# A decoder layer on one core: the last pair of W_down column blocks done in two pieces by tokens, x1's transposes taken in pairs, one weight split moved

## The chip, the core and the metric

One core of a Trainium2 chip runs the whole layer in one launch. The metric is the device time in microseconds of one execution, the median of several runs. The engines are TensorE (PE, with its weight loads shown apart as PEld), VectorE (DVE), ScalarE (ACT), GpSimd (POOL) and SyncE (SP), each with its own instruction stream; they meet only at semaphores.

## The reference, cut to what matters

There are 256 prompt tokens and 8 x 8 sample tokens, 320 in all (TOK), a width of 2048 and a hidden width of 8192, everything in float32. The part that the change touches is the end of the layer:

```python
x = x + rmsnorm(mix, norm_post_mix[i])                                   # x1
hid = jnp.square(jax.nn.relu(rmsnorm(x, norm_pre_mlp[i]) @ w_up[i]))
x = x + rmsnorm(hid @ w_down[i], norm_post_mlp[i])                       # the outputs y_prompt, y_sample
```

`rmsnorm` divides each token by the root of the mean of its squares over all 2048 columns, so nothing of a token's output can be formed before every column of `hid @ w_down` is there for that token. Ahead of these lines stand the two head groups (an SSD scan and a convolution group) and `mix @ W_out`, which the change leaves alone.

## The kernel before

**Layout.** Activations lie transposed: 128 columns of the model on the partitions, a tile `t` (0 to 15) for each 128 columns, and the 320 tokens along the row. A float32 product is made of three float32r products of a high and a low part: `whi*hi`, `whi*lo`, `wlo*hi`. A weight block of 512 rows by 256 columns is loaded by SP into `raw`, rounded by ACT into `whi` (`split`, `ahead` on ACT), and its rest is formed by DVE in `wlo` (`ahead` on DVE). On PE a `granule` is such a block: two column tiles of 128, four row tiles, three matmuls each, 24 matmuls of 128x128 weights by 320 tokens. A pair of column tiles over K = 2048 (one quarter of the hidden width) is four granules (kq = 0 to 3), 96 matmuls. The MLP runs in four quarters of the hidden width; each has 8 pairs of W_up and 8 pairs of W_down, and DVE adds W_down's results into `ya`.

**The end.** The last pair (tiles 14 and 15) is done as 3 granules and then tile by tile over its last four row tiles (L2343 to L2345), with `tile_used` raised for each tile. DVE adds each tile to `ya` (L1796), ACT squares it into `sqm` (L1237), DVE adds the first to the sum of squares `acc2` (L1800), and PE forms the mean over the columns with one-column matmuls (`mean_rows`, L2351 and L2354), one for each block of 128 tokens and two for the 64 sample tokens. ACT takes the roots (L1240), DVE the reciprocals (L1834). `OUT_BLOCKS` is the order of the ten output blocks: (g, c) is 512 columns of the model by 128 tokens (c = 0, 1), or two column groups of the 64 sample tokens (c = 2). For each, PE turns four (or eight) tiles of the scaled result `yw` into token rows in a PSUM bank (`turn_out`, L2369, L2371), DVE multiplies by the reciprocal and adds x1 (L1838), and SP or ACT stores 256 KB, with c = 2 as two stores of 128 KB.

**The x1 stage.** After W_out and its norm (root `q1` by ACT), DVE forms x1 tile by tile in `mix` (L1720, L1724), ACT its high part `ahi` (L1157), DVE its low part `alo` (L1712). PE runs W_up's first two pairs row tile by row tile (`kk`), behind the transposes of the same x1 tile (`turn_x1`), which give x1's token rows that the end adds. Ahead of them PE issues nine 512-column products of data that it has already (L2248; nothing reads them). ACT copies each pair of turned tiles out of PSUM (`keep_rows`), and takes splits of coming weights in between. After the last tile DVE adds up squares, and with PE's mean (`rms_x1`) forms the second norm's `rb2`; the first hidden tiles follow from it.

Of the kernel before, what the change touches and what calls it, by code (L numbers as in the profile page):

```python
# [29 lines left out]
ALU = mybir.AluOpType  # L30
# [40 lines left out]
OUT_BANKS, COL_BANKS = (4, 5, 6, 0, 1, 2, 3), (7, 0, 1)  # L71
OUT_BLOCKS = ((0, 0), (0, 1), (1, 0), (1, 1), (0, 2), (2, 0), (2, 1), (3, 0), (3, 1), (2, 2))
# [36 lines left out]
def build(nc, x_prompt, x_sample, state_ssm, state_ssd_conv, state_conf, w_in, ssd_conv_w, ssd_conv_b,  # L109
# [3 lines left out]
    with ExitStack() as ctx:  # L113
# [237 lines left out]
        def _(sp):  # L351
# [89 lines left out]

            for k, (g, c) in enumerate(OUT_BLOCKS):
                if c == 0:
                    sp.wait_ge(out_done, k + 1)
                    sp.dma_start(y_prompt[0, 0:P, 512 * g:512 * g + 512], yo[:, 0, 512 * g:512 * g + 512]
                                 ).then_inc(y_out, 16)
                if c == 2:
                    sp.wait_ge(out_done, k + 1)
                    sp.dma_start(y_sample.rearrange("b s d -> (b s) d")[:, 512 * g:512 * (g + 1)],
                                 yo[0:64, 2, 512 * g:512 * g + 512]).then_inc(y_out, 16)  # L450
# [263 lines left out]
        def _(act):  # L714
# [492 lines left out]
            ahead(Q_MLP, 0, 6)  # L1207
# [27 lines left out]
            for n in range(2):  # L1235
                act.wait_ge(last_added, n + 1)
                act.activation(sqm[:, n, :], ya[:, NT - 2 + n, :], ACT.Square).then_inc(sqm_done, 1)  # L1237
            act.wait_ge(rms_mm, 3)
            for c in range(3):
                act.activation(scol[:, c:c + 1], ps[:, COL_BANKS[c], 0:1], ACT.Sqrt, bias=eps[:, 0:1]  # L1240
                               ).then_inc(col_root, 1)
            scaled(NT - 2)
            scaled(NT - 1)
            for k, (g, c) in enumerate(OUT_BLOCKS):
                if c == 1:
                    act.wait_ge(out_done, k + 1)
                    act.dma_start(y_prompt[0, P:SEQ, 512 * g:512 * g + 512], yo[:, 1, 512 * g:512 * g + 512]
                                  ).then_inc(y_out, 16)
                if c == 2:
                    act.wait_ge(out_done, k + 1)  # L1250
                    act.dma_start(y_sample.rearrange("b s d -> (b s) d")[:, 512 * (g + 1):512 * (g + 2)],
                                  yo[64:P, 2, 512 * g:512 * g + 512]).then_inc(y_out, 16)
# [8 lines left out]
        def _(dve):  # L1261
# [472 lines left out]
            for t in range(2, NT):  # L1734
                x1_part(t)
                x1_sum(t)
                if t == 2:
# [47 lines left out]

            def down(q, i, last=False):
                for c in range(8):
                    if not (last and c >= 6):
                        ahead(q_down(q), i, c)
                    if c % 4 == 3 and not (isinstance(q, int) and q == 0):  # L1790
                        p = c // 4
                        if last and p:
                            for n in range(2):
                                dve.wait_ge(tile_used, n + 1)
                                m = ya[:, NT - 2 + n, :]
                                dve.tensor_tensor(m, ps[:, 2 + n, 0:TOK], m, ALU.add).then_inc(last_added, 1)  # L1796
                                if n == 0:
                                    dve.wait_ge(acc_done, 3)
                                    dve.wait_ge(sqm_done, 3)
                                    dve.tensor_tensor(acc2[:, 0, :], acc2[:, 0, :], sqm[:, 0, :], ALU.add  # L1800
                                                      ).then_inc(acc_sum, 1)
                            return
# [28 lines left out]
            for k, (g, c) in enumerate(OUT_BLOCKS):  # L1831
                if k in (0, 1, 4):
                    dve.wait_ge(col_root, c + 1)
                    dve.reciprocal(rcol[:, c:c + 1], scol[:, c:c + 1]).then_inc(rcol_done, 1)  # L1834
                    dve.wait_ge(rcol_done, c + 1)
                dve.wait_ge(ot_trans, k + 1)
                rows_out = yo[:, c, 512 * g:512 * g + 512]
                dve.scalar_tensor_tensor(out=rows_out, in0=ps[:, OUT_BANKS[k % 7], :], scalar=rcol[:, c:c + 1],  # L1838
# [6 lines left out]
        def _(pe):  # L1845
# [414 lines left out]
            def turn_x1(t):  # L2260
                bank, n = (4 if t // 2 % 2 else 6), t % 2
                pe.wait_ge(xp_done, t + 1)
                if t == 2:
                    pe.wait_ge(rq_done, 2)
                if t >= 4 and n == 0:
                    pe.wait_ge(x1_rows, t // 2 - 1)
                for c in range(2):
                    pe.transpose(ps[:, bank, 256 * c + n * P:256 * c + (n + 1) * P], mix[:, t, c * P:(c + 1) * P],
                                 ident[:])
                last = pe.transpose(ps[0:64, bank + 1, n * P:(n + 1) * P], mix[:, t, SEQ:TOK], ident[:])  # L2270
                if n:
                    last.then_inc(x1_trans, 1)

            pe.wait_ge(read_dve, 16)
            pe.wait_ge(rooted, 7)
            for c in range(3):
                rows_c = min(P, TOK - c * P)
                last = pe.transpose(ps[0:rows_c, 5, c * P:(c + 1) * P], q1[:, c * P:c * P + rows_c], ident[:])
            last.then_inc(rq_trans, 1)
            for kq in range(4):  # L2280
# [3 lines left out]
                for k in range(4):  # L2284
                    kk = 4 * kq + k
                    turn_x1(kk)
# [43 lines left out]
            for i in range(1, 4):  # L2330
                for p in range(2):
                    pe.wait_ge(read_dve, 32 + 2 * i + p - 1)
                    for kq in range(4):
                        if i == 3 and p and kq == 3:
                            break
                        granule(q_down(3) + 2 * i + p, kq, 2 * p, hhi, hlo)

            pe.wait_ge(lo_done[3], q_down(3) + 8)
            for n in range(2):
                for k in range(4):  # L2340
                    kk = 12 + k
                    wh, wl = whi[:, 3, k, n * P:(n + 1) * P], wlo[:, 3, k, n * P:(n + 1) * P]
                    pe.matmul(ps[:, 2 + n, 0:TOK], wh, hhi[:, kk, :], start=False, stop=False)  # L2343
                    pe.matmul(ps[:, 2 + n, 0:TOK], wh, hlo[:, kk, :], start=False, stop=False)
                    last = pe.matmul(ps[:, 2 + n, 0:TOK], wl, hhi[:, kk, :], start=False, stop=(kk == NT - 1))  # L2345
                last.then_inc(tile_used, 1)


            def mean_rows(squares, first, stop):
                for c in range(2):  # L2350
                    pe.matmul(ps[:, COL_BANKS[c], 0:1], squares[:, c * P:(c + 1) * P], mean1[:, 0:1],  # L2351
                              start=first, stop=stop)
                for h in range(2):
                    last = pe.matmul(ps[64 * h:64 * h + 64, COL_BANKS[2], 0:1], squares[:, SEQ:TOK], mean1[:, 0:1],  # L2354
                                     start=first, stop=stop)
                return last

            def turn_out(k):
                g, c = OUT_BLOCKS[k]
                if k >= 7:  # L2360
# [54 lines left out]
```

## Time and profile before

| | |
|---|---|
| median of 3 runs | 1769.32 us (1769.3 to 1769.61) |
| the profiled execution, its own time | 1768.9 us |
| its span, first to last instruction | 1767.3 us |
| PE busy | 1755.0 us, 99% of the span, 13152 matmuls |
| DVE busy | 1080.9 us (61%) |
| ACT busy | 765.0 us (43%) |
| POOL busy | 451.9 us (26%) |
| granted TensorE clock, mean | 1.000 |

The time is about 1.6 us longer than the span. A matmul's busy time is its latency from start to end; matmuls overlap, so what one costs in a stream is the distance from start to start (or from end to end), and "PE 99% busy" doesn't say that PE is at its peak.

### The profile page before, as it was taken

How to read it: one execution, taken by the hardware profiler on the slowest of the kernel's cores; microseconds unless marked ns; L12 is line 12 of the kernel's file. 1: busy time of each engine (PE TensorE's matmuls, PEld its weight loads, DVE VectorE, ACT ScalarE, POOL GpSimd, SP SyncE). 2: the span in 40 equal slices, each digit the busy share in tenths (PEclk: the TensorE clock that was granted, in tenths of full speed). 3: DMA queues.
4: the chain of work that ended last, by engine and by line, in shares of the span. 5: the costliest groups of instructions: out<-in, count | busy, mean ns of one | idle time of the engine just before them, and what ended most of it. 6: DMA issues, size and time to landing. Idle time of an engine off the chain costs nothing.

```text
span 1767.3 us, 34687 instructions
## 1 busy us (share of the span) xinstructions
PE 1755.0 (99%) x13152; PEld 1732.5 (98%) x13152; DVE 1080.9 (61%) x1972; ACT 765.0 (43%) x1106; POOL 451.9 (26%) x347
## 2 busy tenths in 40 slices
PE   8999999999999999999999999999999999999998
PEld 7999999999999999999999999999999999999998
DVE  5587867999779788865854333444434434344444
ACT  7443435555348566533743333333233333333332
POOL 1577676777652112233100000000000000000232
PEclk9999999999999999999999999999999999999999
DMA  8665554555556777755444544444444444444742
GB/s 247 194 186 159 146 155 139 157 145 146 167 153 185 229 232 228 232 162 159 145 155 148 167 149 153 145 143 149 156 138 158 152 152 143 143 143 153 225 151 91
DMA packets 293608, 290.71 MB, mean 164 GB/s; under 512 B 12678, under 2 KB 287918, under 8 KB 292384
## 3 DMA queue, kind: packets, MB, share of 16 engines
q1 hardware_dynamic: 268008, 257.31, 47.9%
q10 hardware_dynamic: 22512, 19.23, 3.5%
q0 software_dynamic: 2992, 12.84, 2.3%
q8 instruction: 67, 1.10, 0.3%
q14 instruction: 29, 0.24, 0.0%
HBM read 270.85 MB, written 19.93 MB: 165 GB/s over the span
## 4 chain that ended last, share of the span: by engine, by line
PE 94%; DVE 3%; ACT 1%; issue 1%; DMA 0%; DVEq 0%; ACTq 0%
PE ps L1854 29%; PE ps L1856 28%; PE ps L1855 28%; DVE wlo L1266 1%; PE ps L2132 1%; PE ps L2148 1%; PE ps L2173 1%; PE ps L2167 1%; PE ps L2206 1%; PE ps L2208 1%; PE ps L2207 1%; PE ps L1942 0%; PE ps L1941 0%; PE ps L1940 0%; PE ps L2157 0%
## 5 line engine op out<-in xcount | busy, mean ns | idle before, releaser
L1854 PE MATMUL ps<-ahi,whi 128*128 128x320 f32 x2272 | 709.0, 312 | 0.5 <-DVE wlo L1266 0.5
L1856 PE MATMUL ps<-ahi,wlo 128*128 128x320 f32 x2272 | 703.1, 309 | 0.0
L1855 PE MATMUL ps<-alo,whi 128*128 128x320 f32 x2272 | 703.0, 309 | 0.0
L728 ACT ACTIVATE whi<-raw 128x1024 fp32r<-128x1024 f32 x463 | 478.5, 1055 | 399.3 <-PE ps L1856 378.7
L1266 DVE TENSOR_TENSOR wlo<-raw,whi 128x1024 fp32r<-128x1024 f32 x344 | 426.2, 1262 | 225.3 <-ACT whi L728 223.9
L1854 PEld LDWEIGHTS ps<-ahi,whi 128*128 128x128 f32 x2272 | 426.8, 188 | 2.8 <-DVE wlo L1266 0.8
L1855 PEld LDWEIGHTS ps<-alo,whi 128*128 128x128 f32 x2272 | 426.9, 188 | 0.5
L1856 PEld LDWEIGHTS ps<-ahi,wlo 128*128 128x128 f32 x2272 | 426.7, 188 | 0.0
L1856 PE MATMUL ps<-hhi,wlo 128*128 128x320 f32 x1016 | 314.5, 310 | 0.0
L1854 PE MATMUL ps<-hhi,whi 128*128 128x320 f32 x1016 | 314.5, 310 | 0.0
L1855 PE MATMUL ps<-hlo,whi 128*128 128x320 f32 x1016 | 314.4, 309 | 0.0
L539 POOL TENSOR_TENSOR wlo<-raw,whi 128x1024 fp32r<-128x1024 f32 x119 | 284.6, 2411 | 96.7 <-ACT whi L728 96.2
L1423 DVE SCALAR_TENSOR_TENSOR ps<-vx,par,ps 128x256 f32<-128x256 f32 (+1 forms) x928 | 290.7, 382 | 8.1 <-ACT vx L798 7.6
L692 POOL DMA_DIRECT2D yo<-x_rows x1 | 0.7, 737 | 757.5 <-PE ps L1856 757.5
L1855 PEld LDWEIGHTS ps<-hlo,whi 128*128 128x128 f32 x1016 | 190.8, 188 | 0.0
L1856 PEld LDWEIGHTS ps<-hhi,wlo 128*128 128x128 f32 x1016 | 190.8, 188 | 0.0
L1854 PEld LDWEIGHTS ps<-hhi,whi 128*128 128x128 f32 x1016 | 190.8, 188 | 0.0
L1173 ACT ACTIVATE hs<-rh 128x640 f32<-128x640 f32 x32 | 23.6, 739 | 205.3 <-DVE rh L1772 205.3
L1772 DVE SCALAR_TENSOR_TENSOR rh<-ps,rb 128x640 f32<-128x640 f32 x32 | 26.4, 824 | 136.2 <-PE ps L1856 136.2
L1805 DVE TENSOR_TENSOR ya<-ps,ya 128x640 f32 (+1 forms) x23 | 19.0, 824 | 111.0 <-PE ps L1856 111.0
L1775 DVE TENSOR_TENSOR hlo<-hs,hhi 128x640 f32 (+1 forms) x32 | 26.4, 825 | 57.4 <-ACT hhi L1175 57.4
L1854 PE MATMUL ps<-ghi,whi 128*128 128x320 f32 x192 | 59.3, 309 | 0.0
(334 smaller groups left out, 1604.2 us busy)
## 6 DMA issues: line engine op xcount, KB each, us to landing
raw<-in_w_in SPq DMA_DIRECT2D x144, 512.0 KB, 3.7
raw<-in_w_up SPq DMA_DIRECT2D x128, 512.0 KB, 4.3
raw<-in_w_down SPq DMA_DIRECT2D x128, 512.0 KB, 4.5
raw<-in_w_out SPq DMA_DIRECT2D x64, 512.0 KB, 4.2
h<-in_state_ssm ACTq DMA_DIRECT2D x16, 512.0 KB, 5.0
out<-hout SPq DMA_DIRECT2D x16, 512.0 KB, 3.8
wgt<-running_sums ACTq DMA_DIRECT2D x16, 320.0 KB, 5.4
x_transposed<-xt ACTq DMA_DIRECT2D x1, 2560.0 KB, 13.7
```

The lines of the kernel that those rows point to most:

```text
L539: pool.tensor_tensor(wlo[:, kq, :, :], raw[:, kq, :, :], whi[:, kq, :, :].bitcast(F32), ALU.subtract).then_inc(lo_done[kq], 1)
L728: act.activation(whi[:, kq, :, 0:width], raw[:, kq, :, 0:width], ACT.Copy).then_inc(hi_done, 1)
L1173: act.activation(hs[:], rh[:], ACT.Square).then_inc(hs_done, 1)
L1266: dve.tensor_tensor(wlo[:, kq, :, 0:width], raw[:, kq, :, 0:width], whi[:, kq, :, 0:width].bitcast(F32), ALU.subtract).then_inc(lo_done[kq ...
L1423: ins = dve.scalar_tensor_tensor(out=acc[s] if k else src[s], in0=src[s], scalar=par[:, j, R_CONV + k:R_CONV + k + 1], in1=acc[s], op0=ALU ...
L1772: dve.scalar_tensor_tensor(out=rh[:], in0=ps[:, bank:bank + 2, 0:TOK], scalar=0.0, in1=rbb, op0=ALU.max, op1=ALU.mult).then_inc(rh_done, 1)
L1775: dve.tensor_tensor(hlo[:, ds(4 * i + 2 * p, 2), :], hs[:], hhi[:, ds(4 * i + 2 * p, 2), :].bitcast(F32), ALU.subtract).then_inc(hid_ready, 1)
L1805: dve.tensor_tensor(m, gemm_bank(p), m, ALU.add).then_inc(read_dve, 1)
L1854: pe.matmul(out, wh, hi[:, kk, :], start=(kk == 0), stop=False)
L1855: pe.matmul(out, wh, lo[:, kk, :], start=False, stop=False)
L1856: last = pe.matmul(out, wl, hi[:, kk, :], start=False, stop=(kk == NT - 1))
L2132: last = pe.transpose(ps[:, 6 + b // 4, (b % 4) * P:(b % 4 + 1) * P], h0[:, j % 2, b, :], ident[:])
```

## The change

1. The last pair of W_down is done as two pieces. The first takes tokens 128 to 319 (192 of them, `EARLY`) over all four kq, the second tokens 0 to 127 (`LATE`) over all four kq, with the same weights loaded again. Sums, squares, mean and root are done for each piece. `OUT_BLOCKS` is put in another order: blocks of the early tokens first. The early tokens' mean and the blocks k = 0, 1, 2 are put between the late piece's kq, block 3 and the late mean behind it.
2. `turn_x1` takes two tiles at the odd `kk`, and `q1`'s transposes go from ahead of `kk` = 0 to ahead of `kk` = 1. DVE's two reciprocals for them move from tile 2 to tile 3.
3. ACT's split number 6 of W_up goes from behind the tile loop to its last tile, ahead of `keep_rows(6)`.

```diff
-OUT_BANKS, COL_BANKS = (4, 5, 6, 0, 1, 2, 3), (7, 0, 1)
-OUT_BLOCKS = ((0, 0), (0, 1), (1, 0), (1, 1), (0, 2), (2, 0), (2, 1), (3, 0), (3, 1), (2, 2))
+OUT_BANKS, COL_AT = (4, 5, 6, 2, 3, 4, 5, 6, 0, 1), (16, 0, 8)
+OUT_BLOCKS = ((0, 1), (1, 1), (2, 1), (0, 2), (3, 1), (0, 0), (1, 0), (2, 0), (2, 2), (3, 0))
+LATE, EARLY = slice(0, P), slice(P, TOK)
...
+                if t == NT - 1:
+                    ahead(Q_MLP, 0, 6)
                 if t % 2 and t >= 3:
                     keep_rows(t // 2 - 1)
...
-            ahead(Q_MLP, 0, 6)
             ahead(Q_MLP, 0, 7)
...
+            last_squares(0)
+            for k in range(3):
+                store_rows(k)
+            last_squares(1)
+            store_rows(6)
+            store_rows(9)
...
+            def last_part(h):
+                cols = (EARLY, LATE)[h]
+                for n in range(2):
+                    dve.wait_ge(tile_used, 2 * h + n + 1)
+                    m = ya[:, NT - 2 + n, cols]
+                    dve.tensor_tensor(m, ps[:, (2, 0)[h] + n, cols], m, ALU.add).then_inc(last_added, 1)
+                    if n == 0:
+                        dve.wait_ge(acc_done, 3)
+                        dve.wait_ge(sqm_done, 3 + 2 * h)
+                        dve.tensor_tensor(acc2[:, 0, cols], acc2[:, 0, cols], sqm[:, 0, cols], ALU.add
+                                          ).then_inc(acc_sum, 1)
...
-            pe.wait_ge(rooted, 7)
-            for c in range(3):
-                rows_c = min(P, TOK - c * P)
-                last = pe.transpose(ps[0:rows_c, 5, c * P:(c + 1) * P], q1[:, c * P:c * P + rows_c], ident[:])
-            last.then_inc(rq_trans, 1)
...
-                    turn_x1(kk)
+                    if kk == 1:
+                        turn_q1()
+                    if kk % 2:
+                        turn_x1(kk // 2)
                     pe.wait_ge(ahi_done, 2 * NT + kk + 1)
...
+            def last_piece(h, kq):
+                cols = (EARLY, LATE)[h]
+                for n in range(2):
+                    out = ps[:, (2, 0)[h] + n, cols]
+                    for k in range(4):
+                        kk = 4 * kq + k
+                        wh, wl = whi[:, kq, k, n * P:(n + 1) * P], wlo[:, kq, k, n * P:(n + 1) * P]
+                        pe.matmul(out, wh, hhi[:, kk, cols], start=(kk == 0), stop=False)
+                        pe.matmul(out, wh, hlo[:, kk, cols], start=False, stop=False)
+                        last = pe.matmul(out, wl, hhi[:, kk, cols], start=False, stop=(kk == NT - 1))
+                    if kq == 3:
+                        last.then_inc(tile_used, 1)
...
+            pe.wait_ge(read_dve, 32 + 6)
+            for kq in range(4):
+                pe.wait_ge(lo_done[kq], q_down(3) + 8)
+                last_piece(0, kq)
+            pe.wait_ge(read_dve, 32 + 7)
+            last_piece(1, 0)
+            mean_rows(0)
+            last_piece(1, 1)
             turn_out(0)
             turn_out(1)
+            last_piece(1, 2)
             turn_out(2)
+            last_piece(1, 3)
+            turn_out(3)
+            pe.wait_ge(col_root, 2)
+            mean_rows(1)
+            for k in range(4, 10):
                 turn_out(k)
```

PE's stream at the end of the program before, from the last W_down matmul on; a row is a line of the code, the operation, out<-in, the output's shape and what it waits for.

```order
L2345 MATMUL ps<-hhi,wlo 128x320
L2351 MATMUL ps<-mean_95,acc_133 128x1 [waits acc_sum]
L2351 MATMUL ps<-mean_95,acc_133 128x1
L2354 MATMUL ps<-mean_95,acc_133 64x1 x2
L2369 MATMUL ps<-ident,ywa 128x128 [waits yw_done]
L2369 MATMUL ps<-ident,ywa 128x128 x3
L2351 MATMUL ps<-mean_95,sqm 128x1 [waits sqm_done]
L2351 MATMUL ps<-mean_95,sqm 128x1
L2354 MATMUL ps<-mean_95,sqm 64x1 x2
L2369 MATMUL ps<-ident,ywa 128x128 x8
L2369 MATMUL ps<-ident,ywa 128x128 [waits col_root,last_added]
```

The same stream of the changed kernel, where the late piece (128 tokens) ends.

```order
L2371 MATMUL ps<-hhi,wlo 128x128
L2402 MATMUL ps<-ident,ywa 64x128 [waits last_added]
L2402 MATMUL ps<-ident,ywa 64x128 x7
L2381 MATMUL ps<-mean_95,acc_133 128x1 [waits sqm_done,acc_sum,col_root]
L2381 MATMUL ps<-mean_95,sqm 128x1
L2400 MATMUL ps<-ident,ywb 128x128 [waits yw_done]
L2400 MATMUL ps<-ident,ywb 128x128 x3
L2400 MATMUL ps<-ident,ywa 128x128 [waits out_done]
L2400 MATMUL ps<-ident,ywa 128x128 x3
```

Four output blocks (k = 0 to 3) and the early tokens' mean are issued before the late mean; behind it stand the six blocks 4 to 9, where before all ten stood behind or beside the one mean.

PE's stream at the start of the x1 stage, before the change.

```order
L2248 MATMUL ps<-ghi 128x512 x8
L2278 MATMUL ps<-ident,q_138 128x128 [waits rooted,read_dve]
L2278 MATMUL ps<-ident,q_138 128x128
L2278 MATMUL ps<-ident,q_138 64x128
L2268 MATMUL ps<-ident,mix 128x128 [waits xp_done,lo_done1,lo_done0]
L2268 MATMUL ps<-ident,mix 128x128
L2270 MATMUL ps<-ident,mix 64x128
L2293 MATMUL ps<-ahi,whi 128x320 [waits ahi_done]
```

The same place in the changed kernel; left out at the dots are the rest of the first W_up matmuls (`kk` = 0), which alternate L2318 and L2319.

```order
L2267 MATMUL ps<-ghi 128x512 x8
L2318 MATMUL ps<-ahi,whi 128x320 [waits lo_done1,ahi_done,lo_done0,read_dve]
...
L2324 MATMUL ps<-alo,whi 128x320 x3
L2298 MATMUL ps<-ident,q_138 128x128 [waits rooted]
L2298 MATMUL ps<-ident,q_138 128x128
L2298 MATMUL ps<-ident,q_138 64x128
L2289 MATMUL ps<-ident,mix 128x128 [waits xp_done]
```

The six transposes that stood between the nine products and the first W_up matmul are now behind `kk` = 0, so that this matmul's wait for `ahi` stands right behind the nine products.

ACT's stream after the last x1 tile, before the change.

```order
L1143 ACTIVATE sqx<-mix 128x1280
L1151 ACTIVATE rows_86<-ps,sx 128x256 [waits rq_done,x1_trans]
L1151 ACTIVATE rows_86<-ps,sx 128x256
L1152 ACTIVATE rows_86<-ps,sx 64x256
L728 ACTIVATE whi<-raw 128x1024 [waits raw_ready0,weights_used,pst_out,hout_out]
L728 ACTIVATE whi<-raw 128x1024 [waits weights_used,raw_ready1]
```

And in the changed kernel: the first of the two splits has gone ahead of the three row copies.

```order
L1147 ACTIVATE sqx<-mix 128x1280
L732 ACTIVATE whi<-raw 128x1024 [waits weights_used,raw_ready0]
L1155 ACTIVATE rows_86<-ps,sx 128x256 [waits rq_done,x1_trans]
L1155 ACTIVATE rows_86<-ps,sx 128x256
L1156 ACTIVATE rows_86<-ps,sx 64x256
L732 ACTIVATE whi<-raw 128x1024 [waits raw_ready1,weights_used,pst_out,hout_out]
```

## Rows read from the trace of the kernel before

**Rows 1.** The page: span, and PE's busy time, share, instructions.

```profile
span 1767.3 us, 34687 instructions
PE 1755.0 (99%) x13152; PEld 1732.5 (98%) x13152; DVE 1080.9 (61%) x1972; ACT 765.0 (43%) x1106; POOL 451.9 (26%) x347
```

**Rows 2.** The page: the chain that ended last, by engine.

```profile
PE 94%; DVE 3%; ACT 1%; issue 1%; DMA 0%; DVEq 0%; ACTq 0%
```

**Rows 3.** PE's timeline, last pair's kq 3, matmul 1 and 24: start, duration.

```profile
1750.00 0.31 PE L2343 MATMUL ps<-hhi,whi 128*128 128x320 f32 x1
...
1753.37 0.31 PE L2345 MATMUL ps<-hhi,wlo 128*128 128x320 f32 x1
```

**Rows 4.** Weight loads: timeline, then groups (mean ns), then one line's (min/median/max).

```profile
1753.61 0.52 PEld L2351 LDWEIGHTS ps<-mean,acc 128*128 128x128 f32 x4 [0.19 <-DVE acc L1800]
...
L1854 PEld LDWEIGHTS ps<-hhi,whi 128*128 128x128 f32 x1016 | 190.8, 188 | 0.0
...
L2268 PEld LDWEIGHTS ps<-ident,mix x32: 138/140/144, 845.2 to 876.6; 128*128 128x128 f32 x32
...
L1885 PEld LDWEIGHTS ps<-zeros,identb x36: 97/132/152, 3.3 to 14.6; 128*128 128x128 bf16 x36
```

**Rows 5.** Line L2116: loads and matmuls with 64 moving columns, ns min/median/max.

```profile
L2116 PEld LDWEIGHTS ps<-xb,pad x8: 192/192/193, 547.2 to 686.3; 128*128 128x128 f32 x8
L2116 PE MATMUL ps<-xb,pad x8: 222/248/276, 547.3 to 686.4; 128*128 128x64 f32 x8
```

**Rows 6.** PE's timeline behind the last W_down matmul.

```profile
1753.61 0.61 PE L2351 MATMUL ps<-mean,acc 128*128 128x1 f32 x4
1754.14 0.28 PE L2354 MATMUL ps<-mean,acc 128*64 128x1 f32 x4
1754.36 0.66 PE L2369 MATMUL ps<-ident,ywa 128*128 128x128 f32 x4
...
1756.98 1.58 PE L2371 MATMUL ps<-ident,ywa 128*64 128x128 f32 x16
```

**Rows 7.** DVE's timeline there: last add, first reciprocal, last six blocks.

```profile
1753.72 0.49 DVE L1796 TENSOR_TENSOR ya<-ps,ya 128x320 f32<-128x320 f32 x1 [0.17 <-PE ps L2345]
1756.00 0.16 DVE L1834 RECIPROCAL rcol<-scol 128x1 f32<-128x1 f32 x1 [1.78 <-ACT scol L1240]
...
1759.22 4.04 DVE L1838 SCALAR_TENSOR_TENSOR yo<-ps,rcol,yo 128x512 f32<-128x512 f32 x6
```

**Rows 8.** Stores: the first two (1756 to 1758), the last two (from 1763.2).

```profile
out<-yo SPq DMA_DIRECT2D x1, 256.0 KB, 2.3
...
out<-yo SPq DMA_DIRECT2D x1, 128.0 KB, 3.0
out<-yo ACTq DMA_DIRECT2D x1, 128.0 KB, 3.6
```

**Rows 9.** Start of the x1 stage: PE's first transposes, ACT's first tile.

```profile
845.01 0.49 PE L2278 MATMUL ps<-ident,q 128*128 128x128 f32 x3
...
844.80 0.56 ACT L1157 ACTIVATE ahi<-mix,par 128x320 fp32r<-128x320 f32 x1 [0.20 <-DVE mix L1724]
```

**Rows 10.** PE's one wait after the x1 stage.

```profile
900.76 0.31 PE L1856 MATMUL ps<-ahi,wlo 128*128 128x320 f32 x1
901.58 0.41 PE L1854 MATMUL ps<-ahi,whi 128*128 128x320 f32 x1 [0.51 <-DVE wlo L1266]
```

**Rows 11.** ACT after its last x1 tile, and what DVE waits for there.

```profile
874.47 0.81 ACT L1151 ACTIVATE rows<-ps,sx 128x256 f32<-128x256 f32 x2
...
875.54 2.00 ACT L728 ACTIVATE whi<-raw 128x1024 fp32r<-128x1024 f32 x2
...
876.62 1.23 DVE L1266 TENSOR_TENSOR wlo<-raw,whi 128x1024 fp32r<-128x1024 f32 x1 [1.23 <-ACT whi L728]
```

**Rows 12.** The second norm's mean on PE and DVE's step that needs it.

```profile
882.24 1.24 PE L2257 MATMUL ps<-sqx,mean 128*128 128x320 f32 x4
...
884.41 0.49 DVE L1760 SCALAR_TENSOR_TENSOR qq<-qq,ps 128x320 f32<-128x320 f32 x1
```

More of the change, by code:

```diff
@@ L1792, in down @@
                         if last and p:
[L1793 to L1801, printed above, removed]
+                            last_part(0)
                             return
@@ L2258, in rms_x1, with turn_x1, turn_q1 @@
                 last.then_inc(rms_mm, 1)
[L2260 to L2263, printed above, removed]
+            def turn_x1(r):
+                bank = 4 if r % 2 else 6
+                pe.wait_ge(xp_done, 2 * r + 2)
+                if r == 1:
                     pe.wait_ge(rq_done, 2)
[L2265 to L2272, printed above, removed]
-            pe.wait_ge(read_dve, 16)
-            pe.wait_ge(rooted, 7)
-            for c in range(3):
-                rows_c = min(P, TOK - c * P)
-                last = pe.transpose(ps[0:rows_c, 5, c * P:(c + 1) * P], q1[:, c * P:c * P + rows_c], ident[:])
-            last.then_inc(rq_trans, 1)
+                if r >= 2:
+                    pe.wait_ge(x1_rows, r - 1)
+                for n in range(2):
+                    t = 2 * r + n
+                    for c in range(2):
+                        pe.transpose(ps[:, bank, 256 * c + n * P:256 * c + (n + 1) * P], mix[:, t, c * P:(c + 1) * P],
+                                     ident[:])
+                    last = pe.transpose(ps[0:64, bank + 1, n * P:(n + 1) * P], mix[:, t, SEQ:TOK], ident[:])
+                last.then_inc(x1_trans, 1)
+            def turn_q1():
+                pe.wait_ge(rooted, 7)
+                for c in range(3):
+                    rows_c = min(P, TOK - c * P)
+                    last = pe.transpose(ps[0:rows_c, 5, c * P:(c + 1) * P], q1[:, c * P:c * P + rows_c], ident[:])
+                last.then_inc(rq_trans, 1)
+            pe.wait_ge(read_dve, 16)
             for kq in range(4):
@@ L2330, in _ @@
             for i in range(1, 4):
-                for p in range(2):
+                for p in range(2 if i < 3 else 1):
                     pe.wait_ge(read_dve, 32 + 2 * i + p - 1)
                     for kq in range(4):
-                        if i == 3 and p and kq == 3:
-                            break
                         granule(q_down(3) + 2 * i + p, kq, 2 * p, hhi, hlo)
[L2338 to L2346, printed above, removed]
@@ L2349, in mean_rows @@
[L2349 to L2356, printed above, removed]
+            def last_piece(h, kq):
+                cols = (EARLY, LATE)[h]
+                for n in range(2):
+                    out = ps[:, (2, 0)[h] + n, cols]
[7 more added lines that the diff above has]
+                        last.then_inc(tile_used, 1)
@@ new lines, in mean_rows @@
+            def mean_rows(h):
+                pe.wait_ge(acc_sum, h + 1)
+                pe.wait_ge(sqm_done, 4 + 2 * h)
+                for c in ((1, 2), (0,))[h]:
+                    for rows in ((slice(0, P),) if c < 2 else (slice(0, 64), slice(64, P))):
+                        for squares, first in ((acc2[:, 0, :], True), (sqm[:, 1, :], False)):
+                            last = pe.matmul(ps[rows, 7, COL_AT[c]:COL_AT[c] + 1], squares[:, c * P:min(c * P + P, TOK)],
+                                             mean1[:, 0:1], start=first, stop=not first)
+                last.then_inc(rms_mm, 1)
@@ L2358, in turn_out @@
             def turn_out(k):
                 g, c = OUT_BLOCKS[k]
[L2360 to L2361 removed]
+                if k in (3, 8):
+                    pe.wait_ge(last_added, 2 if k == 3 else 4)
+                if k in (5, 6, 7):
+                    pe.wait_ge(out_done, k - 4)
+                if k in (0, 4, 9):
+                    pe.wait_ge(yw_done, {0: 12, 4: NT, 9: NT + 2}[k])
                 for h in range(2 if c == 2 else 1):
@@ L2365, in turn_out @@
                         rows, lo = (slice(0, P), c * P) if c < 2 else (slice(64 * h, 64 * h + 64), SEQ)
-                        out = ps[rows, OUT_BANKS[k % 7], n * P:(n + 1) * P]
+                        out = ps[rows, OUT_BANKS[k], n * P:(n + 1) * P]
                         tile = yw[t // 12][:, t % 12, lo:lo + rows.stop - rows.start]
```

75 lines of the change are left out of this document (33 added, 42 removed).

## The prediction

> **What bounds the kernel now.** I read the page's head first, then the chain that ended last, then timelines of the two stretches that the change touches. PE is busy 99% of the span with 13152 matmuls, each with a weight load of its own [rows 1], and 94% of the chain is PE's, 3% DVE's [rows 2]. So an edit is worth what it adds to or takes from PE's stream, plus what it does in two places where PE isn't the bound: behind the last W_down matmul, and at the one wait after the x1 stage. The last pair's stream has no gap: the 24 matmuls of kq 3 start from 1750.00 to 1753.37, (1753.37 - 1750.00)/23 = 0.1467 us apart, for 320 columns [rows 3]; the pair's 96 take 14.08 us.
>
> **Part 1a, the pair's stream.** The change makes 192 matmuls of these 96: 96 with 192 columns, 96 with 128. It moves the same number of columns, but loads each weight tile twice. If only columns cost, 0.1467 us falls in proportion, to 0.088 and 0.0587 us, and the sum is 14.08 us again. The other bound is the weight load. The mean's matmuls have one column, so nothing of theirs streams, and yet their four loads of 128 columns start 0.11 us apart: (0.52 - 0.19)/3 [rows 4]. A second place has 64 moving columns behind 128-column weights [rows 5]: of its two matmuls the first takes 222 ns, its weights loaded behind a longer matmul, the second 276, 54 ns more, which is the load that it waits for. Both places have plain float32 weights, and the pair's are float32r; but a load of `whi` takes 188 ns, as theirs do (190 and 192), while the loads of the transposes take 140 [rows 4, 5]. At 320 columns a load of 0.11 us is hidden under 0.147 us; at 192 (0.088) and at 128 (0.059) it isn't. I take 0.110 us for both widths, since those rows are the nearest: one has fewer columns than either piece, and the price didn't fall. 192 x 0.110 = 21.1 us against 14.08: **+7.0 us**. Bounds: 0 (columns alone) and, if a narrow matmul kept the whole 0.1467 us, 28.2 - 14.1 = +14.1 us.
>
> The Trainium skill, "TensorE: Matmul & The Clock Gate", section "Weight-path perf modes", says that weights of 128 columns that are not FP32 are read in four parallel chunks, for a load of some 32 cycles. If float32r counted as such, the first term would be 0 and not +7.0 us. The trace speaks against it: bf16 loads took as little as 97 ns, the float32r loads 188 [rows 4]. Its section "Back-to-back issue gap" gives a sustained 81 ns per matmul of 128 columns; by that the term would be an estimated 96 x (0.088 + 0.081) - 14.08 = +2.1 us. No row here shows a 128-column load that quick in a stream.
>
> **Part 1b, what is put between.** The early tokens' mean comes before the late kq 1: four instructions with 128-column weights (1753.61 to 1754.14, 0.53 us) and eight with 64-column ones, whose four took 0.22 us (1754.14 to 1754.36) [rows 6], so 0.44: **+1.0 us**. Blocks 0, 1, 2 are twelve transposes; three `q` ones took 0.49 us with 0.27 for the last [rows 9], so 0.11 each: **+1.3 us**. These ran behind the last W_down matmul before, in DVE's shadow; now they delay it. Waits inside the pieces: the early results are added about 0.35 us after their last matmul, and squares and sums (0.5 us each at 320 columns [rows 7]) finish some 1.5 us into the late kq 0, which takes 24 x 0.11 = 2.6 us. So PE shouldn't wait, and DVE, which is otherwise idle there, does blocks 0 to 2 under the pieces. If that cover went, the wait would be under 1 us. Loads for the pair are split long before. Sum of 1a and 1b: the last W_down matmul starts 9.3 us later relative to the pair's start.
>
> **Part 1c, the tail.** Let T be the start of that last matmul. Before, the last block ends at 1759.22 + 4.04 = 1763.26 with T = 1753.37: T + 9.9 [rows 3, 7]. After: block 3 (16 instructions, 1.58 us [rows 6]) runs from T + 0.15, so PE is free at T + 1.7. The adds and squares of 128 columns are done by then (T + 0.35, then two steps of about 0.3 us and PE's notice: about T + 1.1). The late mean is only 4 instructions, 0.53 us: T + 2.3. Root and reciprocal: T + 2.8. Block 4 needs no late root; its transposes come behind the late mean, T + 2.8, and DVE does it from T + 2.95. Then five blocks: six in a row took 4.04 us, 0.74 for the last, so 0.66 each [rows 7]. With the reciprocal (0.2) between blocks 4 and 5, DVE would end at T + 7.2. Block 8 (sample tokens, 1.6 us of PE) ends its turning about T + 5.8, which costs DVE some 0.15 more. End T + 7.35: **-2.5 us**. Bounds -3.2 (no wait on PE) and -2.0 (each turn late).
>
> Then the drain: from 1763.26 to the span's end 4.04 us. The last stores took 3.0 and 3.6 us to land, the first only 2.3 [rows 8]: the ten blocks' 2.6 MB queue up. After, four blocks are stored earlier, but the last six still come each 0.66 us, so most of the queue stays: **-0.3 us** (0 to -0.9).
>
> **Parts 2 and 3, the x1 stage.** Before, PE starts `q1`'s transposes at 845.01 and x1's behind them [rows 9], work that fills the time until `ahi`'s first tile is there, 844.80 + 0.56 = 845.36. After, the first thing behind the nine products is the matmul that needs this tile: PE starts at about 845.42, 0.4 us late, with all the same work to do. Pairing the transposes saves nothing that I can price. But the chain then goes through DVE and ACT, not PE: at 901.58 PE starts after a wait for `wlo`; it had been ready at 900.76 + 0.147 = 900.91, so 0.67 us was idle [rows 10]. A PE that is 0.4 us late has only 0.27 idle left, if the chain stays. And part 3 shortens the chain: DVE waited 1.23 us for the split that ACT began at 875.54, behind row copies from 874.47 [rows 11]; ahead of them it is 1.07 us sooner. DVE's step at 884.41 needs the mean of which the last of 4 instructions ends at 882.24 + 1.24 = 883.48 [rows 12], 883.9 with PE's delay, so 0.5 us of that is kept. The `wlo` is then ready at 901.08, PE at 901.32, and PE sets it: 901.58 becomes 901.3, **-0.3 us**. Bounds: -0.7 (no idle and no delay), +0.4 (the chain not shortened and PE pushed on in full). Row copies end later by the split's 1.07 us, about 876.6; PE needs them only after the tile loop. Alone, the x1 edits would be within 0.2%.
>
> **The sum.** +7.0 + 1.0 + 1.3 - 2.5 - 0.3 - 0.3 = +6.2 us. Against the profiled execution's own time, 1768.9 us, that is 1775.1. The median of the runs is 0.4 us above that execution, so I predict 1775.5 us, 0.35% slower. A measurement of this kernel tells about 0.2% (3.5 us) from no change.
>
> **The rivals.**
>
> A, the weight load hides or is cheap: pairs stay at the column price, term 1a is 0, and the time is 1775.5 - 7.0 = 1768.5 us, not slower. For it: streams here have no visible load cost at 320 columns, and float32r isn't shown narrow in any row. Against it: rows 4 and 5. It decides if the mean distance of the 192 matmuls is under 0.096 us (192 x 0.0958 = 18.4; less 14.1 and less 0.8 of the other terms is 3.5 us). To be faster by 0.2% it would need the best bounds of tail, drain and x1 stage as well, and cheaper fillers (-0.7, -0.6, -0.4 from 1768.5 is 1766.8, still inside 0.2%). By the 81 ns of the Trainium skill's page on TensorE the time would be an estimated 1775.5 - 7.0 + 2.1 = 1770.6 us. Chance 0.11, of which 0.03 faster.
>
> B, a narrow float32r matmul costs no less than a wide one (0.1467 us), from load and stream not overlapping well: 1775.5 + 7.1 = 1782.6 us. For it: nothing is seen at these widths. Against: one column or 64 cost 0.11 in all. Chance 0.06.
>
> C, the forecast: load-bound at 0.107 to 0.115 us, and the other terms within their bounds: 1773.5 to 1777.5 us. Chance 0.83.
>
> **How the numbers follow.** Range 1772.5 to 1780.5 us: it holds C with a margin for fillers or waits that I have wrong, and the way up towards B (a distance of up to 0.135 us); A is left out. Faster 0.03, same 0.09, slower 0.88.
>
> **What would show it.** In the trace after: the 192 matmuls' starts (or ends) 0.11 us apart in both pieces, and 21 us for the 192 where they are back to back; if the 128-column ones are quicker than the 192-column ones, A is right in part. The last W_down matmul some 9 us later, the last block 7.4 us behind it. PE starting W_up at 845.4 with an idle stretch behind the nine products, and no wait near 901. Wrong above all would be the load's price for float32r, which the trace has only under wide matmuls; next the count of what is hidden behind the late mean.

## The result, and the profile after

The changed kernel takes 1776.57 us, median of 6 runs (1775.52 to 1779.09), against 1769.51 us before in the same session (1769.3 to 1770.13): ratio 1.0043, with a 95% interval of 1.0032 to 1.0054 (the ratios are the recorded ones and need not be the quotient of the medians, here 1.0040). It is slower, as predicted (1775.5, range 1772.5 to 1780.5). Three of the six executions took 1775.52 to 1775.69 us, at a mean granted clock of 1.000, and three 1777.45 to 1779.09, at 0.998 to 0.996. Executions that were disturbed as a whole (two of e2's twelve, at 1891 and 4433 us, and one of the kernel before, at 3483 us) are left out of every comparison. The profiled execution took 1775.52 us. It stands 6.6 us above the profiled one of before; the sum had +6.2.

The page of the changed kernel, head and chain, answers to [rows 1, 2]:

```profile
span 1773.7 us, 34887 instructions
PE 1762.3 (99%) x13248; PEld 1739.7 (98%) x13248; DVE 1081.8 (61%) x1975; ACT 765.9 (43%) x1110; POOL 451.9 (25%) x347
...
PE 98%; DVE 1%; DMA 0%; ACT 0%; issue 0%; SPq 0%; DVEq 0%
```

PE has 96 matmuls more and is busy 7.3 us longer, in a span that is 6.4 us longer. The chain is now 98% PE's: DVE's share at the end and near 901 us has shrunk, and PE's own stream has grown by more.

The two pieces. First the windows (PE, PEld, DVE, ACT, POOL busy, granted clock, DMA share, GB/s): the early piece, then the late one with what is put between.

```profile
1739.29:1749.95 10.66, 10.66 (x98) 10.66 (x97) 3.83 (x5) 2.42 (x5) 5.38 (x3) 1.00 0.01 2
1750.00:1762.72 12.72, 12.72 (x122) 12.69 (x121) 3.35 (x8) 1.77 (x6) 0.00 (x0) 1.00 0.17 63
```

Then the groups by shape (busy us, mean ns of one):

```profile
L2370 PE MATMUL ps<-hlo,whi 128*128 128x128 f32 x32 | 8.8, 274 | 0.0
L2370 PE MATMUL ps<-hlo,whi 128*128 128x192 f32 x32 | 8.8, 274 | 0.0
```

PE never pauses, at the full clock, and a matmul of 128 columns lasts as long as one of 192 (274 ns). The starts tell what one costs. These are the first and the last matmul of the early piece, then the first and the 24th of the late one:

```profile
1739.31 0.25 PE L2369 MATMUL ps<-hhi,whi 128*128 128x192 f32 x1
...
1749.90 0.27 PE L2371 MATMUL ps<-hhi,wlo 128*128 128x192 f32 x1
1750.01 0.24 PE L2369 MATMUL ps<-hhi,whi 128*128 128x128 f32 x1
...
1752.55 0.27 PE L2371 MATMUL ps<-hhi,wlo 128*128 128x128 f32 x1
```

(1749.90 - 1739.31)/95 = 0.111 us for 192 columns and (1752.55 - 1750.01)/23 = 0.110 us for 128, two thirds of the columns; the median distance is 0.111 us in both pieces. For [rows 3] it was 0.1467 us.

PE's timeline at the end, from the last W_down matmul, answers to [rows 6]:

```profile
1762.72 0.27 PE L2371 MATMUL ps<-hhi,wlo 128*128 128x128 f32 x1
1762.92 1.58 PE L2402 MATMUL ps<-ident,ywa 128*64 128x128 f32 x16
1764.43 0.38 PE L2381 MATMUL ps<-mean,acc 128*128 128x1 f32 x2
1764.68 0.36 PE L2381 MATMUL ps<-mean,sqm 128*128 128x1 f32 x2
1764.90 0.63 PE L2400 MATMUL ps<-ident,ywb 128*128 128x128 f32 x4
1765.37 1.47 PE L2400 MATMUL ps<-ident,ywa 128*128 128x128 f32 x12
```

And DVE's there, which answers to [rows 7]:

```profile
1763.03 0.29 DVE L1803 TENSOR_TENSOR ya<-ps,ya 128x128 f32<-128x128 f32 x1 [0.31 <-PE ps L2371]
1763.24 0.15 DVE L1853 RECIPROCAL rcol<-scol 128x1 f32<-128x1 f32 x1
1764.61 0.75 DVE L1857 SCALAR_TENSOR_TENSOR yo<-ps,rcol,yo 128x512 f32<-128x512 f32 x1 [1.22 <-PE ps L2402]
1765.57 0.75 DVE L1857 SCALAR_TENSOR_TENSOR yo<-ps,rcol,yo 128x512 f32<-128x512 f32 x1 [0.21 <-PE ps L2400]
1766.24 0.15 DVE L1853 RECIPROCAL rcol<-scol 128x1 f32<-128x1 f32 x1
1766.43 3.38 DVE L1857 SCALAR_TENSOR_TENSOR yo<-ps,rcol,yo 128x512 f32<-128x512 f32 x5
```

With T = 1762.72 the last block ends at 1766.43 + 3.38 = 1769.81, T + 7.09 (before T + 9.9). The reader can see the plan work as meant: block 3 covers adds and squares (1762.92 to 1764.4), the late mean has only four matmuls, and six blocks are left behind it. The span ends 3.9 us after the last block. The last stores (KB each, median us to landing) are as slow as those of [rows 8]:

```profile
out<-yo SPq DMA_DIRECT2D x2, 128.0 KB, 3.3
...
out<-yo ACTq DMA_DIRECT2D x1, 256.0 KB, 3.5
```

Counted from the pair's start (1739.31 us, before 1739.44), the spans differ by the last W_down matmul 9.5 us later, a tail shorter by 2.8, a drain shorter by 0.1, and 0.1 from the x1 stage: 6.4 us.

The x1 stage: PE's timeline at its start and where the wait of [rows 10] was.

```profile
845.57 0.39 PE L2318 MATMUL ps<-ahi,whi 128*128 128x320 f32 x1 [0.35 <-ACT ahi L1161]
...
901.41 0.31 PE L1875 MATMUL ps<-ahi,wlo 128*128 128x320 f32 x1
901.55 0.31 PE L1873 MATMUL ps<-ahi,whi 128*128 128x320 f32 x1
```

And DVE's timeline where it waited 1.23 us before [rows 11], and at the step of [rows 12]:

```profile
876.19 1.23 DVE L1278 TENSOR_TENSOR wlo<-raw,whi 128x1024 fp32r<-128x1024 f32 x1 [0.16 <-ACT whi L732]
...
884.24 0.49 DVE L1772 SCALAR_TENSOR_TENSOR qq<-qq,ps 128x320 f32<-128x320 f32 x1 [0.30 <-PE ps L2276]
```

PE is idle 0.35 us behind the nine products, and the matmuls near 901 follow each other at 0.147 us with no wait. DVE's wait for the split has gone from 1.23 to 0.16 us, but its step at 884.24 comes only 0.17 us sooner than before, since it now waits for PE's mean.

### The profile page after: what moved, and what is told of

Same layout as the page of the kernel before. It is cut to its first block, busy times and chain, and to the rows that moved or that the text cites. A ratio compares the mean times of both kernels' runs of the same rounds, so it can differ in the third digit from the quotient of the medians.

```text
span 1773.7 us, 34887 instructions
## 1 busy us (share of the span) xinstructions
PE 1762.3 (99%) x13248; PEld 1739.7 (98%) x13248; DVE 1081.8 (61%) x1975; ACT 765.9 (43%) x1110; POOL 451.9 (25%) x347
## 4 chain that ended last, share of the span: by engine, by line
PE 98%; DVE 1%; DMA 0%; ACT 0%; issue 0%; SPq 0%; DVEq 0%
PE ps L1873 29%; PE ps L1874 29%; PE ps L1875 29%; PE ps L2151 1%; PE ps L2167 1%; PE ps L2192 1%; PE ps L2186 1%; PE ps L2318 1%; PE ps L2225 1%; PE ps L2324 1%; PE ps L2226 1%; PE ps L2227 1%; PE ps L2319 1%; PE ps L1961 0%; PE ps L1959 0%; PE ps L1960 0%
## 5 line engine op out<-in xcount | busy, mean ns | idle before, releaser
L1873 PE MATMUL ps<-hhi,whi 128*128 128x320 f32 x992 | 306.5, 309 | 0.0
L1874 PE MATMUL ps<-hlo,whi 128*128 128x320 f32 x992 | 306.5, 309 | 0.0
L1875 PE MATMUL ps<-hhi,wlo 128*128 128x320 f32 x992 | 306.5, 309 | 0.0
L1873 PEld LDWEIGHTS ps<-hhi,whi 128*128 128x128 f32 x992 | 186.2, 188 | 0.0
L1874 PEld LDWEIGHTS ps<-hlo,whi 128*128 128x128 f32 x992 | 186.2, 188 | 0.0
L1875 PEld LDWEIGHTS ps<-hhi,wlo 128*128 128x128 f32 x992 | 186.2, 188 | 0.0
L1875 PE MATMUL ps<-ghi,wlo 128*128 128x320 f32 x192 | 59.2, 308 | 0.0
```

Of the source, the lines that this page charges most:

```text
L1873: pe.matmul(out, wh, hi[:, kk, :], start=(kk == 0), stop=False)
L1874: pe.matmul(out, wh, lo[:, kk, :], start=False, stop=False)
L1875: last = pe.matmul(out, wl, hi[:, kk, :], start=False, stop=(kk == NT - 1))
```

## The experiments

The first three take the change apart.

**e1: part 1 alone** (the two pieces and the new order of the end; x1 stage and split as before).

> Part 1 alone (pieces, tail), the x1 stage as before. Load theory: the whole loss is here, +6.2 to +6.7 us on before, about 1776 us where the granted clock is full; 192 narrow matmuls 0.111 us apart. Rival, the x1 edits cost something of their own: then this is nearer to before, under +5 us. On the executions of the changed kernel that had a mean granted clock of 0.996 to 0.998: if the clock falls because of the narrow stretch, they turn up here and not in e2; if it falls because of PE's idle stretch at 845 us, they turn up in e2 and not here.

Measured: 1776.66 us (1775.65 to 1783.96, 6 runs), ratio 1.0049 (1.0036 to 1.0063), the changed kernel's time. Span 1774.2 us, tail T + 7.1, and the wait near 901 is there as before. All of the loss is in part 1. So are the executions with a lower mean clock: three of the six lie above 1777 us, at 0.994 to 0.998, as three of the changed kernel's do, while the ten of e2 all lie between 1768.72 and 1769.54 us.

**e2: parts 2 and 3 alone** (the x1 stage and the split; the end as before).

> Parts 2 and 3 alone (pairs of transposes, split moved), the end as before. Forecast of the prediction: PE starts W_up 0.4 us late and no longer waits near 901 us: -0.1 to -0.3 us, 1769.2 to 1769.4, not to be told from no change. Rival: the x1 stage carries part of the +6 us; then over +1 us here.

Measured: 1769.25 us (10 runs) against 1769.55, ratio 0.9999 (0.999 to 1.0008), not to be told from no change. PE idles 0.33 us ahead of 845.47, and the wait near 901 is gone. The expected -0.3 us was met, but the next two runs show that its parts weren't.

**e3: part 3 alone.**

```diff
+                if t == NT - 1:
+                    ahead(Q_MLP, 0, 6)
                 if t % 2 and t >= 3:
                     keep_rows(t // 2 - 1)
...
-            ahead(Q_MLP, 0, 6)
             ahead(Q_MLP, 0, 7)
```

> Part 3 alone (the split one place sooner). Chain theory: DVE's steps from 876 us on come 0.5 to 1.0 us sooner, PE is not late, so its idle 0.67 us at 901 us shrinks to under 0.2: -0.5 us, about 1769.0. Rival: the mean at 882 us, which PE gives when it gets there, holds DVE anyway and only 0.4 to 0.5 us comes out; or nothing, if another wait takes its place.

Measured: 1768.57 us (1768.05 to 1768.87, 11 runs) against 1769.55, ratio 0.9995 (0.9986 to 1.0004). DVE's timeline in it:

```profile
883.65 0.49 DVE L1761 SCALAR_TENSOR_TENSOR qq<-qq,ps 128x320 f32<-128x320 f32 x1 [0.28 <-PE ps L2258]
...
899.53 4.63 DVE L1267 TENSOR_TENSOR wlo<-raw,whi 128x1024 fp32r<-128x1024 f32 x4
```

The step of [rows 12] comes 0.76 us sooner and is then held by PE, the `wlo` at 899.53 as much sooner (before 900.30), and PE doesn't wait any more: its 0.67 idle microseconds are all saved, and the span is 1766.6 us, 0.7 shorter. The medians differ by 0.98 us; where the other 0.3 us lies isn't shown. It is the fastest kernel of this study, below both others, though its interval doesn't tell it from no change.

**e6: part 2 alone** (transposes in pairs, `q1`'s behind `kk` = 0; split 6 where it was).

```diff
+                    if kk == 1:
+                        turn_q1()
+                    if kk % 2:
+                        turn_x1(kk // 2)
-                    turn_x1(kk)
```

> Part 2 alone (transposes of x1 in pairs, q1's behind the first row tile). PE 0.4 us late at 845 us; the chain of DVE and ACT unchanged, so the wait near 901 us shrinks from 0.67 to about 0.3 us and the time stays: 0.0 us. Rival: the delay is passed on in full, +0.4 us; or pairing saves on PE, -0.2 us or more.

Measured: 1769.98 us (1769.39 to 1770.58, 11 runs) against 1769.4, ratio 1.0003 (0.9994 to 1.0012): +0.6 us, where nothing was expected; the interval doesn't tell it from no change. The profiled span grew by 0.5 us, and the traces show how. ACT's timeline, first of this kernel:

```profile
854.28 1.06 ACT L728 ACTIVATE whi<-raw 128x1024 fp32r<-128x1024 f32 x1 [0.60 <-PE ps L2305]
```

then of the kernel before:

```profile
853.64 1.06 ACT L728 ACTIVATE whi<-raw 128x1024 fp32r<-128x1024 f32 x1
```

And PE's timeline of this kernel, where the wait of [rows 10] was at 901.58:

```profile
902.22 0.41 PE L1854 MATMUL ps<-ahi,whi 128*128 128x320 f32 x1 [0.51 <-DVE wlo L1266]
```

PE begins the row tile `kk` = 3 at 852.47 us, 0.63 us later than before (851.84), and not 0.4; 0.07 of that was there ahead of the stage. The delayed PE frees its weights later, ACT's split waits for that (0.60 us, where it didn't wait before), and everything that ACT and DVE do from there is 0.64 us later, down to the `wlo` at 900.94 (before 900.30). So PE's delay doesn't eat its idle time near 901: the chain moves with it, and the wait stays 0.5 us long.

The next two measure the price of a narrow matmul.

**e4: each of 92 of the pair's 96 matmuls issued as two, 192 and 128 columns, with the same weights right behind each other**; everything else as before.

```diff
+                        for w, h in ((wh, hhi), (wh, hlo), (wl, hhi)):
+                            first, end = kk == 0 and w is wh and h is hhi, kk == NT - 1 and w is wl
+                            for cols in ((slice(0, TOK),) if first or end else
+                                         (slice(0, WIDTHS[kq]), slice(WIDTHS[kq], TOK))):
+                                last = pe.matmul(ps[:, 2 + n, cols], w, h[:, kk, cols],
+                                                 start=first, stop=end)
```

> The kernel before, with 92 of the last pair's 96 matmuls each issued as two that follow one another with the same weights, 192 and 128 columns; nothing else is changed, results are the same. Load theory: 184 x 0.111 + 4 x 0.147 - 14.1 = +6.9 us, about 1776.4. Rival 1, columns are the price: 0. Rival 2, a repeated weight tile is not loaded again: about 0 as well, or half of it (92 loads fewer). Rival 3, the loss of the change comes from what is put between the pieces and from the tail: 0 here.

Measured: 1776.38 us (1776.01 to 1776.69, 5 runs), ratio 1.004 (1.0026 to 1.0053); the last W_down matmul 7.2 us later (7.0 counted from the pair's start), the tail 9.9 us as before. The price goes with the number of matmuls and their loads, whatever the order, and weights that are already there are loaded and paid for again: the trace has 92 weight loads more than before.

**e5: the same with other widths, one for each kq**: 256 + 64, 192 + 128, 160 + 160, 288 + 32.

```diff
-            WIDTHS = (192, 192, 192, 192)
+            WIDTHS = (256, 192, 160, 288)
```

> As e4, but the split of the columns differs by kq: 256+64, 192+128, 160+160, 288+32. Load theory, a matmul starts no sooner than 0.111 us after the one before, and no sooner than 0.000458 us a column: 256 gives 0.117, 288 gives 0.132, all others 0.111 (64 and 32 too). Column theory: 0.029 for 64, 0.015 for 32. A theory of a fixed cost per matmul on top of the columns: 0.088 + x and 0.059 + x differ in the same granule, which the load theory says they don't. Its time (about 1776.8) is of no interest.

Measured: 1777.4 us (one run). From the starts, two matmuls of a pair together take 227, 223, 223 and 244 ns. In groups by shape (the mean of one is its latency):

```profile
L2349 PE MATMUL ps<-hhi,whi 128*128 128x160 f32 x16 | 3.1, 276 | 0.0
...
L2349 PE MATMUL ps<-hlo,whi 128*128 128x288 f32 x8 | 3.0, 379 | 0.0
...
L2349 PE MATMUL ps<-hlo,whi 128*128 128x64 f32 x8 | 1.5, 192 | 0.0
...
L2349 PE MATMUL ps<-hhi,whi 128*128 128x32 f32 x8 | 1.4, 178 | 0.0
```

A matmul costs the larger of its columns (0.1467/320 = 0.458 ns each) and 111 ns. For 192 + 128 and 160 + 160 that is 2 x 111 = 222 ns, for 256 + 64 it is 117 + 111 = 228, for 288 + 32 it is 132 + 111 = 243. A price by columns (147 ns for every pair) falls, and so does a fixed extra for each matmul, which would make all pairs equal. A least distance between the starts of any two matmuls falls too: behind a matmul of 32 columns the next one starts 26 to 30 ns later. It is the starts of the weight loads that are never less than 0.108 us apart here. That the number of weight columns sets this shows in [rows 6], for plain float32: four matmuls with 64-column weights took 0.22 us, 0.055 each, half of the 0.11 with 128.

**e7: the split by tokens in the last kq only** (48 narrow matmuls for 24 wide ones, the early mean inside, all ten blocks behind; parts 2 and 3 as in the changed kernel).

> The split by tokens only in the last kq of the last pair: 48 narrow matmuls in place of 24 wide ones, kq 0 to 2 at 320 columns; early mean between the late piece's two tiles, ten output blocks behind the last matmul. Load theory: 48 x 0.111 - 3.5 = +1.8 us in place of +7.2; mean +1.0; the tail ends about 8 us behind the last matmul's start in place of 9.9: sum +0.9 us, 1770.4. Rival, the loss is in the tail's order and the work between: then this is as slow as the change, +4 us or more.

Measured: 1770.81 us (1770.52 to 1773.55, 11 runs), ratio 1.0011 (1.0002 to 1.002). Counted from the pair's start, the last W_down matmul is 2.7 us later (48 x 0.111 - 24 x 0.1467 = 1.8, and the mean's 0.8), the tail 1.1 us shorter. Even a quarter of the split costs more than it gives back. Two of the 11 executions stand apart, at 1773.16 and 1773.55 us, with a mean clock of 0.998 and 0.997; neither was profiled.

**e8: the changed kernel with blocks 0 to 2 behind the last matmul** and not between the late kq.

```diff
             last_piece(1, 1)
+            last_piece(1, 2)
+            last_piece(1, 3)
             turn_out(0)
             turn_out(1)
-            last_piece(1, 2)
             turn_out(2)
-            last_piece(1, 3)
```

> The changed kernel with output blocks 0 to 2 turned behind the last matmul and not between the late pieces. If doing them early gains what the prediction says: the last matmul starts 1.4 us sooner than in the changed kernel, the tail grows by 1.6 us (three blocks of DVE, 0.66 each, less what PE's turning of block 3 and the late mean left idle): +0.2 us on the changed kernel. Rival, they are a net loss where they stand: 1 us faster than the changed kernel. Rival, they hide well: 1 us or more slower.

Measured: 1784.11 us (1778.22 to 1784.89, 5 runs), ratio 1.0073 (1.0059 to 1.0087), 7.5 us above the changed kernel: a plain miss. Four of the five lie above 1782 us, at a mean clock of 0.994 to 0.996, the fifth at 1778.22, at 0.999. The windows of a slower one show what none of the theories had (the granted clock is the third number from the end):

```profile
1749.90:1753.50 3.60, 3.60 (x36) 3.60 (x34) 0.72 (x2) 0.62 (x2) 0.00 (x0) 1.00 0.00 0
1753.50:1756.00 2.50, 2.50 (x21) 2.47 (x21) 0.16 (x1) 1.10 (x4) 0.00 (x0) 0.64 0.00 0
1756.00:1760.00 4.00, 4.00 (x21) 4.00 (x21) 0.00 (x0) 0.00 (x0) 0.00 (x0) 0.50 0.00 0
...
1768.00:1771.30 3.30, 3.30 (x17) 3.30 (x18) 0.81 (x2) 0.00 (x0) 0.00 (x0) 0.50 0.00 0
1771.30:1775.00 3.70, 2.50 (x25) 2.12 (x24) 2.85 (x7) 0.62 (x2) 0.00 (x0) 1.00 0.59 215
```

and its PE timeline:

```profile
1760.10 0.41 PE L2371 MATMUL ps<-hhi,wlo 128*128 128x128 f32 x1
1760.31 0.41 PE L2369 MATMUL ps<-hhi,whi 128*128 128x128 f32 x1
```

PE never pauses, and yet its clock is at the lower of its two levels, 1.2 GHz, from about 1754 to 1771.3 us, with the matmuls 0.213 us apart. Before that fall PE had been issuing narrow matmuls without a pause since the pair's start. So the question became whether the same cost the changed kernel something in its executions above 1777 us. The next two runs test it with one edit in each kernel, which adds no instruction: the late piece streams 192 columns for each load, and what it adds is read by nothing.

```diff
-                cols = (EARLY, LATE)[h]
+                cols = (EARLY, slice(0, 192))[h]
```

**e9: this edit on e8's kernel.**

> The kernel of e8 (the early tokens' mean between the late piece's kq, blocks 0 to 2 behind it), with one more edit: the late piece's 96 matmuls stream 192 columns (tokens 0 to 191) instead of 128. The 64 added columns go to columns of the PSUM banks that nothing reads. Both widths are load-bound at 0.111 us, so at the full clock nothing should change: about 1778.2 us, the one execution of e8 with a mean granted clock of 0.999. Theory (the granted clock of 0.5 in e8 came with the little that 128-column matmuls stream for each load, not with the loads or the length of the unbroken stretch): no stretch at 0.5 in the profile, mean clock 0.999 or 1.0 in nearly all executions, median 1778.2 us (1777.5 to 1779). Rival (any load-bound stretch without other work between, whatever its columns): the clock falls to 0.5 as in e8, with a mean clock of 0.994 to 0.996 and a median near 1784 us.

Measured: 1778.02 us (1776.68 to 1778.55, 5 runs), ratio 1.0046 (1.0032 to 1.0059), 6.1 us less than e8 with 6144 streamed columns more. All executions have a mean clock of 0.998 or 0.999. Its windows over the late piece, then a stretch of the tail:

```profile
1753.50:1756.00 2.50, 2.50 (x26) 2.50 (x23) 0.16 (x1) 1.10 (x4) 0.00 (x0) 1.00 0.00 0
1756.00:1761.60 5.60, 5.60 (x52) 5.60 (x52) 0.00 (x0) 0.00 (x0) 0.00 (x0) 1.00 0.01 3
...
1764.70:1766.20 1.50, 0.00 (x0) 0.01 (x1) 0.92 (x4) 0.62 (x2) 0.00 (x0) 1.00 0.97 347
...
1767.60:1769.00 1.40, 1.40 (x9) 1.40 (x8) 1.30 (x3) 0.08 (x1) 0.00 (x0) 0.50 0.79 181
```

The clock stays at 1.00 through the late piece, with the same loads, 0.111 us apart, in a stretch as long. So neither the loads nor the length of the stretch by itself made it fall in e8; what e8 has otherwise is 64 columns less in each late matmul. Two reservations: there is one profile of each, and e8 ran on another chip than e9 and e10 (the kernel before takes the same on both, 1769.4 and 1769.43 us). In one thing the expectation missed: there is a stretch at 0.5, in the tail from about 1767.1 to 1770.5, behind a pause of PE of 1.6 us that ends at 1766.2. That makes the agreement with 1778.2 partly luck. The two executions at 1776.68 suggest that the order of e8 costs 1.1 us at the full clock; no profile of such an execution was taken.

**e10: this edit on the changed kernel.**

> The changed kernel with the same one edit: the late piece's matmuls stream 192 columns instead of 128. Theory that the 1 us between the changed kernel's median (1776.57) and its executions at a mean clock of 1.0 (1775.6) is the granted clock in the 128-column piece: no execution near 1779 with a mean clock of 0.996, all at 1775.5 to 1775.9, median 1775.7 us. Rival (the clock falls in some executions for another reason, or elsewhere): the same spread up to 1779 us, median near 1776.6. If a 192-column matmul cost more than a 128-column one in the stream, the time would be above 1775.7 in every execution; the trace after has both at 0.111 us.

Measured: 1775.79 us (1775.57 to 1776.0, 5 runs), ratio 1.0036 (1.0022 to 1.005). None of its executions lies above 1776.0 us (the expectation had 1775.9), where the changed kernel and e1 have 6 of 12 above 1777 us, each of these with a mean clock of 0.994 to 0.998. The mean clock alone doesn't tell: two executions of e10 have 0.998, at 1775.96 and 1776.0 us. In the profile of one the clock is at 0.5 in two places, neither of them in the late piece. One is from 10.5 to 13.9 us, at the kernel's start; the other is the second of these windows,

```profile
1768.00:1771.00 3.00, 1.23 (x12) 0.82 (x8) 2.10 (x4) 0.00 (x0) 0.00 (x0) 1.00 0.99 352
1771.00:1775.00 4.00, 0.00 (x0) 0.00 (x0) 0.00 (x0) 0.00 (x0) 0.00 (x0) 0.60 0.48 134
```

the drain, where PE has nothing left to do.

## Why the prediction was right, and where it wasn't

- **Part 1a, right.** The forecast stands or falls with the load's price for float32r: 0.110 us assumed, 0.111 measured at 192 and at 128 columns, so 191 x 0.111 = 21.2 us to the last start for 13.9 before, +7.3 (predicted +7.0). e4 shows it without the rest of the change, e5 that it is the larger of two prices. Rival A (columns alone) and rival B (0.1467 us for every matmul) both fall. The Trainium skill, "TensorE: Matmul & The Clock Gate", section "LDWEIGHTS (loading the stationary operand)", gives a load as its columns divided by 1.2 in ns, 107 for 128; the measured distance of 0.111 us is near that, while the two other sections of that page which the prediction weighed would have given +0 and +2.1 us.
- **Part 1b, right.** What stands between the pieces takes 23.4 - 21.2 = 2.2 us (2.3 predicted), of which the mean is about 0.8. PE waits for nothing in there. The last W_down matmul comes 9.5 us later, 9.3 predicted.
- **Part 1c, right.** The tail gives back 2.8 us (2.5 predicted, bound 3.2), the drain 0.1 and not 0.3, because the last six blocks still come at DVE's pace and their stores queue as before. The gain that the change is after is real; it is a third of what the stream pays.
- **Parts 2 and 3: a small sum of two wrong terms.** -0.3 us predicted. The medians of e2 differ by -0.3, the profiled spans by -0.4, and in the changed kernel's trace the last pair starts 0.13 us sooner. But part 2 costs 0.6 us alone (0.5 in the span) and part 3 gives 1.0 (0.7 in the span). None of the three intervals tells its difference from no change; what carries the account is the steps in the traces. The step that failed is "0.27 idle left, if the chain stays": the chain doesn't stay. ACT's split waits until PE has used the weights, so a late PE makes ACT and DVE late by 0.64 us (e6), and PE was late by 0.6 there and not by 0.4. I had listed what PE waits for in that stage, and not who there waits for PE.
- **The sum.** The terms were off by +0.3 (1a), -0.1 (1b), -0.3 (tail), +0.2 (drain) and +0.2 us (x1 stage). They partly cancel, and that part of the agreement is luck.
- **Not foreseen: the clock.** Executions at a mean clock of 1.0 take 1775.5 to 1775.7 us, what was forecast; the median is 1776.57 since half of them lie above. The range holds it by a margin that was meant for other terms. e8 to e10 speak for the granted clock in the 128-column piece: e8's profile shows it fall there, and with 192 columns for each load neither of the two profiles shows a fall in that piece. That it falls there in the changed kernel's longer executions is inferred: the one that was profiled has the clock at 1.00 up to the drain, and if half of all executions are long, as in the changed kernel and e1, five good ones of e10 would come by chance once in 32 times. A fall in the tail, as e9's profile has it, is the rival that stays open; the two long executions of e7, whose narrow matmuls are a quarter as many, fit it no worse.

## What to carry to other kernels

A matmul in a stream costs the larger of two prices, its columns and its weight load; splitting the columns of a matmul is free only while each part stays above the load, here 0.111/0.000458 = 242 columns, so no split of 320 is free. Before a split by tokens is made for an earlier end, count its matmuls times the gap: here 9.5 us of stream bought 2.9 us of tail, and of the three edits only the three lines that move a split ahead of copies may be worth keeping (1768.57 us, with the wait near 901 gone from the trace). Where an engine on the critical path is made late at one place, look for who waits for it there, before its idle time further on is counted as cover.

## What the runs showed of the hardware that I had not expected

- A PE that never pauses can lose its clock: 1.2 GHz from about 1754 to 1771 us in e8, among back-to-back 128-column matmuls with a load each, and not with 192 columns in the same places (e9). There is one profile of each, on two chips. The same stream costs 0.213 us a matmul at that level and 0.111 at 2.4 GHz, so the load's price nearly doubles as the clock halves.
- With columns added that nobody reads a kernel took 6.1 us less (e8 to e9).
- Weights that are issued again right behind themselves are loaded again (e4: +7.0 us of stream for 92 such loads and their narrow matmuls).
- The latency of a matmul doesn't tell its price. In e4 and e5 a 128-column matmul that shares its weights with a 192-column one has a mean of 244 to 246 ns and the 192-column one 301 to 307, while in two separate pieces both have 274; the distance from start to start is 0.111 to 0.112 us on average in every case.
